# Softmax bias from a minimum of negated logits in four of five attentions

## Chip, core and metric

One NeuronCore of one Trainium2 chip runs the whole kernel. The metric is the device time of one execution in microseconds; lower is better. Three runs of the kernel before gave 2366.38, 2356.47 and 2365.3 us, median 2365.3.

## The reference

The program is two transformer blocks on 512 tokens of width 1024, all in fp32. The first has two layers: latent attention (16 heads, causal), memory cross-attention (4 heads over 256 memory rows) and a gated MLP; then sparse attention (16 heads over the best 128 keys of each query, with a bias by distance), cross-attention and the MLP again. The second block has a gated causal attention (8 heads), a pooling mixer and an MLP with a short convolution. Every attention ends in the same arithmetic for a block of 128 queries:

```
logits = q k^T * scale (+ bias), masked entries -inf
p = exp(logits - max(logits)) / sum(exp(logits - max(logits)))
out = p v
```

## The kernel before

Matrix products of weights are split in a high and a low part and made of three matmuls; they fill most of the program. Each engine has one hand-written stream of instructions, and semaphores order them. The change lies in the five attentions, which have the names `mla` (64 steps), `xa0` and `xa1` (16 steps each), `dsa` (the sparse one, 64 steps) and `fox` (the gated one, 32 steps). A step is one head and one block of 128 queries. Block 0 has 128 keys, block 1 256, block 2 384, block 3 512, so four steps in a row have four widths; the cross-attentions always have 256.

What the engines do for step i, in the order of the work:

- TensorE makes the logits in a PSUM bank (`do_logits`, up to four steps ahead; it waits for `max_done` of the step that used the bank before).
- GpSimd, in `dsa` alone, adds the bias BI and the mask MK into one of two buffers BB (L2305). Its add for step i waits for `max_done` of step i-2 (L2303).
- VectorE, in `maxima` (L1772), adds the mask (or BB) to the logits, writes the sum to the SBUF buffer PB, and reduces it to a maximum MX. This is a custom instruction, out = (in0 op0 in1) * scale with a reduction of out by op1 that starts from a given value; a short read-out instruction then writes MX and raises `max_done`.
- VectorE, in `negate` (L1777), waits for that MX, writes NM = -scale * MX and raises `negmax_done`.
- ScalarE, in `exps` (L1305), waits for `negmax_done` and computes exp(scale * PB + NM) in place, with the row sum in RS.
- VectorE takes the reciprocal RI of the sum (`invert`, L1782), waits for it and multiplies PB by it (`normalise`, L1788).
- TensorE transposes PB (`do_turn`, L775), ScalarE copies the result to SBUF, and TensorE multiplies it with the values (`do_av`, L805 or L974).

VectorE's order within a tick is: invert i, normalise i, maxima i+2, negate i+2, and then a low part of a finished head where there is one. In `dsa`, before the steps 12, 28 and 44, it also copies the keys of the next group (K_D, L2098). Each of MX, NM, RS, RI and PB has four slots, by i % 4; maxima of step i waits until the transposes of step i-4 are done, so slot i % 4 of MX is not written before the exponential of step i-4 has been used.

Of the kernel before, what the change touches and what calls it, by code (L numbers as in the profile page):

```python
# [6 lines left out]
ALU = mybir.AluOpType  # L7
ACT = mybir.ActivationFunctionType
# [7 lines left out]
S, D, MEM = 512, 1024, 256  # L16
# [15 lines left out]
TAKEN = -3.0e38  # L32
# [97 lines left out]
def build_program(nc, A, consts, out):  # L130
    ctx = ExitStack()
    with ctx:
# [32 lines left out]
        MX = keep("MX", [P, 4])  # L165
        NM = keep("NM", [P, 4])
# [162 lines left out]
        max_done = sem("max_done")  # L329
        negmax_done = sem("negmax_done")  # L330
# [68 lines left out]
        def logits_bank(name, i):  # L399
            return bank[i // 2 % 2][:, MEM * (i % 2):] if name[:2] == "xa" else bank[i % 4][:, :]  # L400
# [802 lines left out]
        def _(act):  # L1203
# [92 lines left out]
            def attention(name, groups, heads, scale, out_tile, after=None):  # L1296
                steps = 4 * heads
                s0 = STEP0[name]
                xa = name[:2] == "xa"

                def exps(g, i):
                    w = MEM if xa else P * (i % 4) + P
                    act.wait_ge(negmax_done, g * steps + (s0 + i + 1))
                    pb = PBUF[name][:, i % 4, 0:w]
                    nc.scalar.activation(pb, pb, ACT.Exp, bias=NM[:, i % 4:i % 4 + 1], scale=scale,  # L1305
                                         accum_out=RS[:, i % 4:i % 4 + 1]).then_inc(exp_done, 1)

                def evac(g, i):
                    w = MEM if xa else P * (i % 4) + P
                    act.wait_ge(turned, g * steps + (s0 + i + 1))  # L1310
                    act.wait_ge(av_done, g * steps + (s0 + i - 1))
                    copy(PTB[name][:, i % 2, 0:w], turned_bank(name, i)[:, 0:w]).then_inc(pt_done, 1)

                def outs(g, i):
                    if xa:
                        if i % 4 == 3:
                            act.wait_ge(av_done, s0 + i + 1)
                            for d in range(2):
                                out_tile(0, i // 4 * 2 + d)
                    elif i % 4 == 3:  # L1320
                        act.wait_ge(av_done, g * steps + (s0 + i + 1))
                        out_tile(g, i // 4)

                def tick(at):
                    for op, step in ((exps, at(0)), (evac, at(-2)), (after, at(-3)), (outs, at(-3 if xa else -4))):
                        if step is not None and op is not None:
                            op(*step)
                pipeline(act, groups, steps, 3 if xa else 4, 0, tick)
# [87 lines left out]
            def cross_attention(layer, stage):  # L1416
                proj_and_memory(stage, layer)
                name = f"xa_kv{layer}"

                def kv(first):  # L1420
                    def unit(i, j):
                        v = i + first
                        for k in range(2):
                            t = (TILE0[name] + 2 * j + k) % 4
                            act.wait_ge(tile_ready, v * 2 + (TILE0[name] + k + 1))
                            if first == 0:
                                dst = KX[:, bass.ds(i * 2 + k, 1), :]
                            else:
                                dst = VX[:, k, bass.ds(i * 256, 256)]
                            copy(dst, bank[t][:, 0:MEM]).then_inc(tile_free, 1)  # L1430
                        after_unit(name, v, j, v * 2 + (TILE0[name] + 2))
                    return unit

                def first_unit():
                    act.wait_ge(tile_free, TILE0[name])
                    kv(0)(0, 0)

                def next_units():
                    kv(0)(1, 1)
                    kv(0)(2, 0)  # L1440
                shift = ln(3 * layer, bank[7], later=True, amid=(first_unit, next_units))
                for v in range(3, 8):
                    first = v // 4 * 4
                    kv(first)(v - first, v % 2)
                    for c in KV_CHUNKS[v]:
                        shift(c)
                q = f"xa_q{layer}"

                def queries(i, j):
                    for k in range(2):  # L1450
                        act.wait_ge(tile_ready, i * 2 + (TILE0[q] + k + 1))
                        copy(QX[:, bass.ds(i * 2 + k, 1), :], bank[(TILE0[q] + 2 * j + k) % 4][:, :]).then_inc(tile_free, 1)
                wide_units(q, queries)
                attention(f"xa{layer}", 1, 4, (D // 4) ** -0.5, o_hi)
                for i in range(4):
                    if i in (0, 3):
                        mod_load(MOD_N * layer + i // 3)
                    after_unit(f"xa_o{layer}", i, i, TILE0[f"xa_o{layer}"] + 2 * i + 2)
                ln(3 * layer + 1, bank[7])
# [40 lines left out]
            def dsa_qi(i, j):  # L1500
                for k in range(2):
# [10 lines left out]
                 scale=float(IDXH ** -0.5)).then_inc(tile_free, 1)  # L1512
# [3 lines left out]
            for i in range(4):  # L1516
                w = P * i + P
# [65 lines left out]
                r = head_rows(hh)  # L1583
                copy(QD[r, hh // 2, :], bank[6 + hh % 2][r, :]).then_inc(o_copied, 1)
            act.sem_inc(o_copied, 2)
            attention("dsa", 1, 16, 1.0, o_copy)
            for c in range(DC):
                act.wait_ge(o_copied, 2 + HEADS)
                if c == 0:
# [63 lines left out]
                act.wait_ge(tile_free, TILE0["fox_pool"] + g + 1)  # L1653
                copy(XH[:, 4 + g, :], UF[:, g, :]).then_inc(x_hi, 1)
            after_unit("fox_pool", 0, 0, TILE0["fox_pool"] + 4)
            attention("fox", 1, 8, 0.125, head_hi)
            wide_units("fox_o", nothing)
            rms("rms2", lambda c: (tile_free, TILE0["fox_o"] + c + 1), bank[7], G2, MODC[:, 24:32], True)
            hidden(2)
# [9 lines left out]
        def _(dve):  # L1669
# [90 lines left out]
            def attention(name, groups, heads, scale, bias, out_tile, before=None):  # L1760
                steps = 4 * heads
                s0 = STEP0[name]
                xa = name[:2] == "xa"

                def maxima(g, i):
                    w = MEM if xa else P * (i % 4) + P
                    pb = PBUF[name][:, i % 4, 0:w]
                    dve.wait_ge(turned, g * steps + (s0 + i - 3))
                    in1 = bias(g, i)
                    dve.wait_ge(logits_ready, g * steps + (s0 + (i // 2 * 2 + 2 if xa else i + 1)))  # L1770
                    dve.sem_inc(logits_seen, 1)
                    nc.vector.tensor_tensor_reduce(pb, logits_bank(name, i)[:, 0:w], in1, 1.0, TAKEN, ALU.add, ALU.max,  # L1772
                                                   MX[:, i % 4:i % 4 + 1]).then_inc(max_done, 1)

                def negate(g, i):
                    dve.wait_ge(max_done, g * steps + (s0 + i + 1))
                    nc.vector.tensor_scalar(NM[:, i % 4:i % 4 + 1], MX[:, i % 4:i % 4 + 1], -scale, None,  # L1777
                                            ALU.mult).then_inc(negmax_done, 1)

                def invert(g, i):  # L1780
                    dve.wait_ge(exp_done, g * steps + (s0 + i + 1))
                    nc.vector.reciprocal(RI[:, i % 4:i % 4 + 1], RS[:, i % 4:i % 4 + 1]).then_inc(rsum_done, 1)  # L1782

                def normalise(g, i):
                    w = MEM if xa else P * (i % 4) + P
                    pb = PBUF[name][:, i % 4, 0:w]
                    dve.wait_ge(rsum_done, g * steps + (s0 + i + 1))
                    nc.vector.tensor_scalar(pb, pb, RI[:, i % 4:i % 4 + 1], None, ALU.mult).then_inc(probs_ready, 1)  # L1788

                def outs(g, i):  # L1790
                    if out_tile is None:
                        return
                    if xa:
                        if i % 4 == 3:
                            for d in range(2):
                                out_tile(0, i // 4 * 2 + d)
                    elif i % 4 == 3:
                        out_tile(g, i // 4)

                def tick(at):  # L1800
                    for op, step in ((before, at(0)), (invert, at(0)), (normalise, at(0)), (maxima, at(LAG)), (negate, at(LAG)),
                                     (outs, at(-4 if xa else -5))):
                        if step is not None and op is not None:
                            op(*step)
                for i in range(LAG):
                    maxima(0, i)
                    negate(0, i)
                pipeline(dve, groups, steps, 4 if xa else 5, LAG, tick)
# [225 lines left out]
            for i in range(NQ * IDXH):  # L2034
                qb, h = divmod(i, IDXH)
                w = P * qb + P
# [316 lines left out]
```

## Time and profile before

| what | value |
|---|---|
| median of three runs | 2365.3 us (2356.47 to 2366.38) |
| the profiled execution | 2371.9 us, span 2370.1 us |
| TensorE busy | 2256.4 us, 95% |
| VectorE busy | 1277.2 us, 54% |
| ScalarE busy | 1017.0 us, 43% |
| GpSimd busy | 185.9 us, 8% |
| granted TensorE clock, mean | 0.98 of full speed |

The span runs from the first to the last instruction of the profiled execution. PE is TensorE's matmul row, PEld its weight loads, DVE VectorE, ACT ScalarE, POOL GpSimd. Busy shares are means over stages with different limits, so a stage is read by its own window. An instruction's length in the timeline includes the time in which it was started but could not go on.

### The profile page before, as it was taken

The page shows a single profiled execution, that of the slowest core. Times are in us where ns is not written, and L with a number is a line of the kernel's source. Part 1 is how long each engine was busy: PE and PEld are TensorE (multiplying, and loading weights), DVE is VectorE, ACT ScalarE, POOL GpSimd, SP SyncE. Part 2 cuts the span into 40 slices and gives each one's busy share as a digit, 9 for nine tenths or more (in the row PEclk, how much of TensorE's full clock was granted, in tenths as well). Part 3 has the DMA queues.
Part 4 walks back from the last instruction along what each step waited for, and adds up shares of the span by engine and source line. Part 5 has one row for each costly group of instructions (what it writes and reads, how often), then busy time and mean ns, then how long its engine had stood idle before and what let it go on. Part 6 is the DMA issues. An engine that isn't in the chain of part 4 may idle for free.

```text
span 2370.1 us, 47335 instructions
## 1 busy us (share of the span) xinstructions
PE 2256.4 (95%) x18750; PEld 2137.4 (90%) x18754; DVE 1277.2 (54%) x2566; ACT 1017.0 (43%) x1576; POOL 185.9 (8%) x200
## 2 busy tenths in 40 slices
PE   7999999899999999788999899999989998999998
PEld 7978999899999888667999899999959897999997
DVE  5477544565652348998444555553254645656412
ACT  4566354433331253766354343332153535555413
POOL 1000300100000210154200100000030000000000
PEclk9999999999999999899999999999999999999999
DMA  6333341355442222000241245553212211333230
GB/s 162 76 100 89 108 142 45 89 137 156 133 151 89 80 79 83 20 1 19 72 160 63 81 116 133 136 150 104 89 45 89 77 37 54 101 94 95 100 106 36
DMA packets 303371, 219.07 MB, mean 92 GB/s; under 512 B 34379, under 2 KB 290321, under 8 KB 303249
## 3 DMA queue, kind: packets, MB, share of 16 engines
q1 hardware_dynamic: 251568, 189.32, 26.7%
q10 hardware_dynamic: 49920, 25.17, 4.1%
q0 software_dynamic: 1760, 2.88, 0.4%
q8 instruction: 87, 1.43, 0.3%
q14 instruction: 36, 0.29, 0.0%
HBM read 207.58 MB, written 2.10 MB: 88 GB/s over the span
## 4 chain that ended last, share of the span: by engine, by line
PE 85%; DVE 6%; ACT 4%; issue 2%; POOL 2%; DMA 0%; DVEq 0%; POOLq 0%; ACTq 0%; SPq 0%
PE bank L654 72%; PE bank L805 2%; PE bank L739 2%; PE bank L775 2%; PE bank L905 1%; PE bank L974 1%; POOL ZS L2239 1%; PE bank L966 1%; DVE PB_D L1772 1%; DVE M L2025 1%; PE bank L1174 1%; POOL BB L2305 1%; PE bank L1108 1%; ACT WH L617 0%; ACT XH L1208 0%
## 5 line engine op out<-in xcount | busy, mean ns | idle before, releaser
L654 PE MATMUL bank<-XH,WH 128*128 128x256 f32 x3568 | 1000.5, 280 | 32.1 <-DVE XL L1887 24.5
L654 PE MATMUL bank<-XL,WH 128*128 128x256 f32 x3568 | 997.3, 280 | 0.0
L654 PE MATMUL bank<-XH,WL 128*128 128x256 f32 x3568 | 997.0, 279 | 0.0
L654 PEld LDWEIGHTS bank<-XH,WH 128*128 128x128 f32 x3568 | 676.4, 190 | 40.6 <-issue 32.3
L654 PEld LDWEIGHTS bank<-XL,WH 128*128 128x128 f32 x3568 | 679.8, 191 | 0.2 <-issue 0.2
L654 PEld LDWEIGHTS bank<-XH,WL 128*128 128x128 f32 x3568 | 675.8, 189 | 0.0
L621 DVE TENSOR_TENSOR WL<-RAW,WH 128x2048 fp32r<-128x2048 f32 x172 | 396.5, 2305 | 514.7 <-ACT WH L617 514.7
L617 ACT ACTIVATE WH<-RAW 128x2048 fp32r<-128x2048 f32 x172 | 328.7, 1911 | 441.9 <-PE bank L654 441.8
L654 PE MATMUL bank<-HH,WH 128*128 (+1 forms) x1056 | 293.3, 278 | 0.9 <-DVE HF L1976 0.9
L654 PE MATMUL bank<-HL,WH 128*128 (+1 forms) x1056 | 293.2, 278 | 0.0
L654 PE MATMUL bank<-HH,WL 128*128 (+1 forms) x1056 | 293.2, 278 | 0.0
L654 PEld LDWEIGHTS bank<-HL,WH 128*128 128x128 f32 x1056 | 199.7, 189 | 0.0
L654 PEld LDWEIGHTS bank<-HH,WH 128*128 128x128 f32 x1056 | 198.2, 188 | 1.1 <-DVE HF L1976 1.1
L654 PEld LDWEIGHTS bank<-HH,WL 128*128 128x128 f32 x1056 | 198.2, 188 | 0.0
L1208 ACT ACTIVATE HH<-HF 128x512 f32 x66 | 41.8, 633 | 142.8 <-DVE HF L1961 107.0
L1961 DVE TENSOR_TENSOR HF<-SG,bank 128x512 f32<-128x512 f32 x44 | 30.3, 688 | 110.6 <-PE bank L654 110.6
L2220 POOL TENSOR_TENSOR ZS<-ZB 128x512 f32<-128x512 f32 x6 | 7.7, 1291 | 1020.4 <-DVE ZB L1992 754.3
L1913 DVE SCALAR_TENSOR_TENSOR ACC<-MB,CA,ACC 128x128 f32<-128x128 f32 x288 | 79.6, 345 | 0.0
L1978 DVE TENSOR_TENSOR HL<-HF,HH 128x512 f32 x66 | 45.7, 692 | 60.9 <-ACT HH L1208 60.9
L1470 ACT ACTIVATE SG<-bank 128x512 f32<-128x512 f32 x44 | 26.4, 599 | 114.1 <-DVE ACCT L1919 109.0
L1842 DVE SCALAR_TENSOR_TENSOR ZB<-XT,bank 128x512 f32<-128x512 f32 x32 | 21.9, 686 | 94.1 <-PE bank L654 94.1
L1470 ACT ACT_TABLE_LOAD x22 | 28.2, 1283 | 99.0 <-DVE ACC L1917 98.7
(311 smaller groups left out, 3255.9 us busy)
## 6 DMA issues: line engine op xcount, KB each, us to landing
RAW<-in_ffn_w_in SPq DMA_DIRECT2D x88, 512.0 KB, 5.1
MB<-in_mod_w ACTq DMA_DIRECT2D x48, 512.0 KB, 5.5
RAW<-in_ffn_w_down SPq DMA_DIRECT2D x44, 512.0 KB, 4.3
RAW<-in_ffn_up SPq DMA_DIRECT2D x44, 512.0 KB, 4.6
RAW<-in_xa_w_kv SPq DMA_DIRECT2D x32, 512.0 KB, 4.4
RAW<-in_ffn_down SPq DMA_DIRECT2D x22, 512.0 KB, 4.2
RAW<-in_xa_w_q SPq DMA_DIRECT2D x16, 512.0 KB, 3.9
RAW<-in_xa_w_o SPq DMA_DIRECT2D x16, 512.0 KB, 4.0
```

The source lines that it names most:

```text
L617: nc.scalar.activation(WH[:, par, :], RAW[:, par, :], ACT.Copy).then_inc(w_hi, 1)
L621: nc.vector.tensor_tensor(WL[:, par, :], RAW[:, par, :], f32(WH[:, par, :]), ALU.subtract).then_inc(w_split, 1)
L654: mm = nc.tensor.matmul(out_ap[:, cols], l, moving, start=(start and n == 0 and k == 0), stop=(stop and n == len(parts) - 1 and k == len(o ...
L739: nc.tensor.matmul(sq_bank[:, :], ONES, SQ[:, c % 4, :], start=(c == 0), stop=(c == DC - 1)).then_inc(sq_summed, 1)
L775: mm = nc.tensor.transpose(turned_bank(name, i)[:, P * kb:P * kb + P], pb[:, i % 4, P * kb:P * kb + P], IDN)
L805: mm = nc.tensor.matmul(o, v(hh, kb), PTB[name][:, i % 2, P * kb:P * kb + P], start=(kb == 0), stop=(kb == qb))
L905: return nc.tensor.matmul(b[:, 0:w], Q_M[hh // 2][0:NOPE + ROPE, hh % 2, P * qb:P * qb + P], K_M[0:NOPE + ROPE, hh, 0:w], start=True, stop ...
L1208: return nc.scalar.activation(dst, src, ACT.Copy, **kw)
L1470: nc.scalar.activation(SG[:, j, :], b0[:, :], ACT.Silu).then_inc(silu_done, 1)
L1913: ins = nc.vector.scalar_tensor_tensor(out=a, in0=MB[:, c, :], scalar=CA[:, c:c + 1], in1=a, op0=ALU.mult, op1=ALU.add)
L1961: nc.vector.tensor_tensor(HF[:, j, :], SG[:, j, :], b1[:, :], ALU.mult).then_inc(tile_free, 2)
L1978: nc.vector.tensor_tensor(HL[:, bass.ds(i, 1), :], HF[:, j, :], f32(HH[:, bass.ds(i, 1), :]), ALU.subtract).then_inc(hid_split, 1)
```

## The change

In all attentions but `mla` the reduction multiplies the sum by -scale instead of 1.0 and takes the minimum instead of the maximum, starting from the positive of the large constant. MX then holds -scale * max, and PB the negated scaled logits. The exponential takes MX as its bias and -1.0 as its factor, and waits for `max_done` instead of `negmax_done`. `negate` does nothing there. `mla` keeps the maximum, the negation and its wait. No buffer, no other wait and no order of other instructions is changed.

```diff
@@ -1300,9 +1300,13 @@
 
                 def exps(g, i):
                     w = MEM if xa else P * (i % 4) + P
-                    act.wait_ge(negmax_done, g * steps + (s0 + i + 1))
+                    if scale is None:
+                        act.wait_ge(max_done, g * steps + (s0 + i + 1))
+                    else:
+                        act.wait_ge(negmax_done, g * steps + (s0 + i + 1))
+                    low, by = (MX, -1.0) if scale is None else (NM, scale)
                     pb = PBUF[name][:, i % 4, 0:w]
-                    nc.scalar.activation(pb, pb, ACT.Exp, bias=NM[:, i % 4:i % 4 + 1], scale=scale,
+                    nc.scalar.activation(pb, pb, ACT.Exp, bias=low[:, i % 4:i % 4 + 1], scale=by,
                                          accum_out=RS[:, i % 4:i % 4 + 1]).then_inc(exp_done, 1)
 
                 def evac(g, i):
@@ -1451,7 +1455,7 @@
                         act.wait_ge(tile_ready, i * 2 + (TILE0[q] + k + 1))
                         copy(QX[:, bass.ds(i * 2 + k, 1), :], bank[(TILE0[q] + 2 * j + k) % 4][:, :]).then_inc(tile_free, 1)
                 wide_units(q, queries)
-                attention(f"xa{layer}", 1, 4, (D // 4) ** -0.5, o_hi)
+                attention(f"xa{layer}", 1, 4, None, o_hi)
                 for i in range(4):
                     if i in (0, 3):
                         mod_load(MOD_N * layer + i // 3)
@@ -1583,7 +1587,7 @@
                 r = head_rows(hh)
                 copy(QD[r, hh // 2, :], bank[6 + hh % 2][r, :]).then_inc(o_copied, 1)
             act.sem_inc(o_copied, 2)
-            attention("dsa", 1, 16, 1.0, o_copy)
+            attention("dsa", 1, 16, None, o_copy)
             for c in range(DC):
                 act.wait_ge(o_copied, 2 + HEADS)
                 if c == 0:
@@ -1653,7 +1657,7 @@
                 act.wait_ge(tile_free, TILE0["fox_pool"] + g + 1)
                 copy(XH[:, 4 + g, :], UF[:, g, :]).then_inc(x_hi, 1)
             after_unit("fox_pool", 0, 0, TILE0["fox_pool"] + 4)
-            attention("fox", 1, 8, 0.125, head_hi)
+            attention("fox", 1, 8, None, head_hi)
             wide_units("fox_o", nothing)
             rms("rms2", lambda c: (tile_free, TILE0["fox_o"] + c + 1), bank[7], G2, MODC[:, 24:32], True)
             hidden(2)
@@ -1769,10 +1773,14 @@
                     in1 = bias(g, i)
                     dve.wait_ge(logits_ready, g * steps + (s0 + (i // 2 * 2 + 2 if xa else i + 1)))
                     dve.sem_inc(logits_seen, 1)
-                    nc.vector.tensor_tensor_reduce(pb, logits_bank(name, i)[:, 0:w], in1, 1.0, TAKEN, ALU.add, ALU.max,
+                    negated = name != "mla"
+                    nc.vector.tensor_tensor_reduce(pb, logits_bank(name, i)[:, 0:w], in1, -scale if negated else 1.0,
+                                                   -TAKEN if negated else TAKEN, ALU.add, ALU.min if negated else ALU.max,
                                                    MX[:, i % 4:i % 4 + 1]).then_inc(max_done, 1)
 
                 def negate(g, i):
+                    if name != "mla":
+                        return
                     dve.wait_ge(max_done, g * steps + (s0 + i + 1))
                     nc.vector.tensor_scalar(NM[:, i % 4:i % 4 + 1], MX[:, i % 4:i % 4 + 1], -scale, None,
                                             ALU.mult).then_inc(negmax_done, 1)
```

## Rows read from the trace of the kernel before

**Rows 1.** The page: busy time by engine (part 1) and the chain that ended last (part 4).

```profile
PE 2256.4 (95%) x18750; PEld 2137.4 (90%) x18754; DVE 1277.2 (54%) x2566; ACT 1017.0 (43%) x1576; POOL 185.9 (8%) x200
...
PE 85%; DVE 6%; ACT 4%; issue 2%; POOL 2%; DMA 0%; DVEq 0%; POOLq 0%; ACTq 0%; SPq 0%
```

**Rows 2.** Busy time by window: first attention, a cross-attention, the sparse one, the gated one.

```profile
core 0: us, PE busy (x) PEld busy (x) DVE busy (x) ACT busy (x) POOL busy (x), PEclk, DMA share, GB/s
134.50:222.40 87.90, 86.87 (x579) 72.78 (x579) 78.10 (x329) 67.36 (x203) 0.00 (x0) 0.97 0.31 84
365.40:399.80 34.40, 32.38 (x226) 30.10 (x227) 21.55 (x87) 18.84 (x55) 0.00 (x0) 1.00 0.10 32
1011.00:1119.00 108.00, 95.23 (x594) 75.21 (x593) 101.24 (x326) 70.27 (x207) 54.66 (x62) 0.99 0.01 1
1869.00:1921.50 52.50, 49.69 (x317) 39.09 (x319) 42.87 (x170) 36.68 (x104) 0.00 (x0) 0.95 0.11 36
```

**Rows 3.** Line L775, the transposes: ns min/median/max, first to last start.

```profile
L775 PE MATMUL bank<-KC,PB_M x160: 272/273/476, 135.0 to 223.0; 128*128 128x128 f32 x160
...
L775 PE MATMUL bank<-KC,PB_D x160: 272/273/330, 1014.3 to 1118.6; 128*128 128x128 f32 x160
```

**Rows 4.** Tile NM: its instructions, and who waited for them (us, times).

```profile
L1777 DVE TENSOR_SCALAR NM<-MX x192: 153/153/156, 133.7 to 1918.5; 128x1 f32<-128x1 f32 x192
...
  ACT PB_D L1305: 38.8, 50
```

**Rows 5.** Timeline, sparse attention: start us, length us, engine, line, instruction [idle <-releaser].

```profile
1045.67 0.08 DVE L1772 DVE_READ_ACCUMULATOR2_ANT MX<- 128x1 f32 x1
1045.78 0.15 DVE L1777 TENSOR_SCALAR NM<-MX 128x1 f32<-128x1 f32 x1
...
1045.85 0.15 DVE L1782 RECIPROCAL RI<-RS 128x1 f32<-128x1 f32 x1
1045.92 1.28 POOL L2305 TENSOR_TENSOR BB<-BI,MK 128x512 f32<-128x512 f32 x1 [0.80 <-DVE MX L1772]
...
1046.04 1.24 DVE L1788 TENSOR_SCALAR PB_D<-PB_D,RI 128x128 f32<-128x128 f32 x1
...
1047.20 0.55 DVE L1772 CUSTOM_DVE_ANT_0 PB_D<-bank,BB 128x384 f32<-128x384 f32 x1
...
1047.67 0.08 DVE L1772 DVE_READ_ACCUMULATOR2_ANT MX<- 128x1 f32 x1
...
1047.94 0.46 POOL L2305 TENSOR_TENSOR BB<-BI,MK 128x128 f32<-128x128 f32 x1 [0.75 <-DVE MX L1772]
...
1048.04 0.50 DVE L1788 TENSOR_SCALAR PB_D<-PB_D,RI 128x256 f32<-128x256 f32 x1
1048.47 0.68 DVE L1772 CUSTOM_DVE_ANT_0 PB_D<-bank,BB 128x512 f32<-128x512 f32 x1
```

**Rows 6.** Groups by shape, sparse attention: count | busy us, mean ns | idle before.

```profile
L1788 DVE TENSOR_SCALAR PB_D<-PB_D,RI 128x128 f32<-128x128 f32 x16 | 16.0, 1000 | 0.6
...
L1788 DVE TENSOR_SCALAR PB_D<-PB_D,RI 128x256 f32<-128x256 f32 x16 | 7.9, 496 | 0.6
```

**Rows 7.** Groups by shape, gated attention: the same columns.

```profile
L1788 DVE TENSOR_SCALAR PB_F<-PB_F,RI 128x256 f32<-128x256 f32 x8 | 2.8, 353 | 0.3
...
L1788 DVE TENSOR_SCALAR PB_F<-PB_F,RI 128x128 f32<-128x128 f32 x8 | 2.3, 286 | 0.3
```

**Rows 8.** Timeline, sparse attention: a move of keys beside an add.

```profile
1031.80 1.82 DVE L2098 COPY K_D<-KD 64x512 f32<-64x512 f32 x2
1031.87 1.46 POOL L2305 TENSOR_TENSOR BB<-BI,MK 128x512 f32<-128x512 f32 x1 [0.80 <-DVE MX L1772]
```

**Rows 9.** Timeline: the start of the first cross-attention.

```profile
369.72 0.08 DVE L1772 DVE_READ_ACCUMULATOR2_ANT MX<- 128x1 f32 x1
...
370.03 0.43 DVE L1772 CUSTOM_DVE_ANT_0 PB_X<-bank,KC 128x256 f32<-128x256 f32 x1
...
370.52 1.59 PEld L966 LDWEIGHTS bank<-KX,QX 128*128 128x128 f32 x8 [1.81 <-DVE MX L1772]
```

## The prediction

> **What bounds the kernel now.** I read the page first: TensorE is busy for 95% of the span and makes 85% of the chain that ended last, VectorE 6% [rows 1]. A small edit on VectorE can matter only where TensorE is not the bound, so the second view is busy time by window [rows 2]. In the first attention TensorE is busy 86.9 of 87.9 us, in a cross-attention 32.4 of 34.4, in the gated one 49.7 of 52.5: TensorE's own work ends last there. The sparse attention is the exception: 95.2 of 108.0 for TensorE, 101.2 for VectorE, 54.7 for GpSimd, which works in none of the others. The transposes show its price: the first and the sparse attention have the same 64 steps and 160 transposes, but those of the first lie between 135.0 and 223.0 us (88.0), those of the sparse one between 1014.3 and 1118.6 (104.3) [rows 3]. So 16.3 us is about the most that any relief of VectorE can bring there. The four attentions that change hold 16 + 64 + 16 + 32 = 128 of the 192 negations [rows 4], half of them in the sparse one.
>
> The third view is the timeline of the sparse attention, to see what a step waits for [rows 5]. After a reduction its read-out MX starts at 1045.67. The negation follows at 1045.78, the reciprocal at 1045.85, the normalisation of 128 columns at 1046.04. That one lasts 1.24 us. GpSimd's add of the bias for a later step was released by the same MX and had started at 1045.92, 0.12 before the normalisation; it ended at 1045.92 + 1.28 = 1047.20, and the normalisation ended at 1047.28. The next reduction starts at 1047.20. It is the same with 256 columns: add 1047.94 to 1048.40, normalisation 1048.04 to 1048.54, next reduction 1048.47. The means say that this is the rule: 1000 and 496 ns in the sparse attention [rows 6], 286 and 353 in the gated one, where GpSimd is idle [rows 7]. So VectorE's 101 us hold stalls: the normalisation and the add want something that only one of them has at a time, and the one that starts first keeps it. The cycle that sets the pace is: MX, 0.25 us to the add, the whole add, 0.08 to the normalisation's end, the next reduction. The negation stands beside the 0.25 us, not in the cycle.
>
> **The change, part by part.** *Negations removed.* Each takes 0.15 us, but the reciprocal starts 0.07 behind it, since they overlap; what it holds up is the wait for MX. From MX's start to the reciprocal it is 0.18 now. Without the negation nothing between them waits for MX (the reciprocal reads the sums of an older step). The nearest spacing shown of two such short instructions is the 0.07 from negation to reciprocal, so I take 0.07 and a gain of 0.11 us of VectorE's order for each step. The bounds are 0 (the read-out holds the engine until the reciprocal starts as now) and 0.18.
>
> *Sparse attention, steady steps.* 0.11 x 64 = 7 us would be the answer if VectorE's own order set the pace. By the cycle above the normalisation only comes earlier to a stall that ends when the add ends: gain 0. What hides it is the add; if that cover goes, the next bounds are TensorE's pace. The condition is that the add still comes first. After MX the add starts at 0.25 (512 columns) and 0.27 (128 columns) [rows 5]; the normalisation comes at 0.37 now and at 0.07 + 0.19 = 0.26 then. So they start level, within 0.01. Who has it then no row shows directly. Two rows bound it: 0.12 behind, the normalisation waits [rows 5]; a copy that starts 0.07 ahead makes the add of 512 last 1.46 instead of 1.28, so it went first [rows 8]. Between these I estimate from the same rows. The adds cost 0.46 and 1.28 us for 128 and 512 columns, so 2.14 ns a column and 0.19 fixed: the add's data start at most 0.19 after its start. The stalled normalisation lost 1.24 - 0.29 = 0.95 us, so, if it could go on when the add ended, it first needed its turn at 1047.20 - 0.95 = 1046.25, that is 0.21 after its start. A common error in the end of the add shifts both alike. So VectorE asks about 0.02 later in its instruction than GpSimd, and must start some 0.02 ahead to win. It does not, narrowly. I take 0 and keep -16.3 as the other end.
>
> *Sparse attention, edges.* Before each of three key moves a copy stands where the reciprocal stands otherwise; it comes 0.11 sooner and lets its add begin sooner: 0.3. The last two steps have no add beside them: 0.2, and the last exponential is not held by the negation: 0.1. Sum 0.6, bounds 0 and 1.2.
>
> *Starts.* In a cross-attention TensorE's fifth step waits for the second reduction, which starts 0.31 after the first MX because the negation lies between [rows 9]. Four attentions x 0.11 = 0.4.
>
> *Steady steps of the cross and gated attentions.* TensorE has 2.0, 2.0 and 2.8 us free in them [rows 2], most of it at their ends: I take 0.3, bounds 0 and 3. ScalarE's exponentials wait for MX instead of NM, 0.19 sooner by the rows (1045.93 + 0.03 against 1045.75 + 0.03). It waited 38.8 us for NM in the sparse one [rows 4], but it had long finished what VectorE reads next, so this costs and gives nothing.
>
> *The reduction with a minimum and a factor that is not 1.* No row shows it. It still reads one PSUM and one SBUF operand and writes the same columns; the nearest row is its own sibling, 0.68 us for 512 and 0.55 for 384 columns [rows 5]. I take the same time. Above, a second pass over the columns at (0.68 - 0.55) / 128 = 1.0 ns each; below, nothing: the time follows the columns already. No DMA, no queue and no wait is added; the wait for MX replaces the one for NM, and behind it in ScalarE's order stands what stood there before.
>
> Sum: 0 + 0.6 + 0.4 + 0.3 = 1.3 us off the profiled execution's 2371.9 (its span is 2370.1). That execution lies 6.6 above the median 2365.3, so on the median's scale it is **2364.0**. A measurement of this kernel can tell about 0.5%, 11.8 us, from no change, and its three runs alone spread over 9.9.
>
> **The rivals.** *A. The order turns for the small add only.* The normalisation of 256 columns starts 0.26 after MX, the add of 128 beside it 0.27 after. If whoever starts first wins, it costs 0.35 instead of 0.50 and starts 0.11 sooner, 0.26 us in each of some 15 rounds of four steps, 3.9 us: 2360.1. For it: the start times. Against it: the 0.02 estimated above. The Trainium skill states this rule (SBUF — State Buffer, Who interferes with whom): VectorE and GpSimd share one port pair, and the one that issues first holds it for its whole instruction. By that rule, taken to the letter, A is the outcome; the stalls in the rows agree with the rule and leave its last 0.02 us open.
>
> *B. The order turns for all adds.* Then the normalisations cost 0.29 to 0.49 and the adds go behind them. The stall goes, but the adds come late and VectorE meets their rest in the next step, and TensorE's pace is close behind. I take half of the 16.3: 8.2, so with the edges 2355.8. For it: they start level. Against it: it needs 0.02 us of lead at the large adds, where 0.01 of lag is expected.
>
> *C, on the other side: the new reduction is slower.* It stands in the pace-setting cycle of the sparse attention. With a second pass it costs on average 320 columns x 1.0 ns = 0.33 us more, x 64 = 21 us: 2385. It decides from 0.18 us a reduction (11.8 / 64). For it: only that no row shows the form. Against it: its sibling already adds, scales and reduces in one pass.
>
> *D. Nothing reaches the end at all*, because the spacing is the read-out's own: 2365.3. It can't be told from my forecast by time, only by the trace.
>
> **How the numbers follow.** Forecast and D together 0.60, A 0.18, B 0.16, C 0.04, other 0.02. The range 2353 to 2369 takes in the forecast, A, B and D with the spread of the median, and leaves out C. Faster by over 0.5% needs B with over 11.8 of its 16.3 us: 0.07. Slower is C and a little drift: 0.04. Within: 0.89.
>
> **What would show it.** Right: L1777 has 64 instructions; the reciprocal starts 0.07 after MX; the normalisations of 128 columns still last about 1.3 us (they start earlier and end with the add); the transposes of the sparse attention still span 104. Wrong: these normalisations fall to 0.3 and the adds grow (B), only those of 256 do (A), or the reduction of 512 columns leaves 0.68 us (C). A spacing far from 0.07 would undo the order argument both ways.

## The result, and the profile after

The changed kernel took 2352.28 us (median of 19 runs, 2339.02 to 2378.91), the kernel before 2374.09 us (median of 19, 2350.78 to 2409.14). The ratio is 0.992, with a 95% interval of 0.9894 to 0.9945: faster by 0.8%, some 19 us of 2374 (13 to 25 by the interval). Ratio and interval leave out the executions that fell into a slower state of the chip (2378.91 us of the changed kernel is one), so the ratio is not quite the quotient of the two medians, 0.991. The profiled execution took 2369.5 us with a span of 2367.7, only 2.4 us less than the one of before. The stage that gained can be read from the trace, and so can much of why these two spans hide it.

The page of the kernel after, busy time by engine and the chain that ended last, against [rows 1]:

```profile
PE 2265.1 (96%) x18750; PEld 2151.4 (91%) x18754; DVE 1250.6 (53%) x2438; ACT 1017.7 (43%) x1576; POOL 190.0 (8%) x200
...
PE 88%; ACT 5%; DVE 3%; issue 2%; POOL 1%; DMA 0%; DVEq 0%; ACTq 0%; SPq 0%; POOLq 0%
```

VectorE's part of the chain is 3% where it was 6%; TensorE's rose from 85% to 88%. Next the windows of a cross-attention, the sparse and the gated attention, with the columns of [rows 2]:

```profile
366.80:401.20 34.40, 32.34 (x225) 30.05 (x226) 19.18 (x71) 19.15 (x56) 0.00 (x0) 1.00 0.10 32
1031.20:1123.00 91.80, 88.95 (x595) 74.05 (x594) 83.06 (x262) 71.75 (x207) 58.11 (x62) 0.98 0.01 1
1861.60:1914.00 52.40, 49.83 (x317) 39.14 (x319) 39.20 (x138) 36.55 (x105) 0.00 (x0) 0.95 0.11 38
```

The cross and the gated attention need what they needed (34.4 and 52.4 us here, 34.4 and 52.5 before). The window of the sparse attention is drawn here from its first reduction; TensorE is busy 89.0 of its 91.8 us. GpSimd is busy 58.1 us, where it was 54.7: its adds now hold the waits. The transposes date the stage more sharply, against [rows 3]:

```profile
L775 PE MATMUL bank<-KC,PB_M x160: 272/273/443, 135.5 to 223.1; 128*128 128x128 f32 x160
...
L775 PE MATMUL bank<-KC,PB_D x160: 272/273/329, 1034.5 to 1122.5; 128*128 128x128 f32 x160
```

In the first attention they span 87.6 us (88.0 before). In the sparse one they span 88.0 us, from 1034.5 to 1122.5, where it was 104.3. The sparse attention now runs at the pace of the first one, and these are the 16.3 us that the prediction put down as about the most that a relief of VectorE could bring (runs 7 and 8 below go 2.9 us further, without the adds).

The timeline of the kernel after shows how, against [rows 5] (start us, length us, engine, line, instruction):

```profile
1066.10 0.07 DVE L1777 DVE_READ_ACCUMULATOR2_ANT MX<- 128x1 f32 x1
1066.10 0.15 DVE L1790 RECIPROCAL RI<-RS 128x1 f32<-128x1 f32 x1
...
1066.29 0.29 DVE L1796 TENSOR_SCALAR PB_D<-PB_D,RI 128x128 f32<-128x128 f32 x1
1066.35 1.82 POOL L2313 TENSOR_TENSOR BB<-BI,MK 128x512 f32<-128x512 f32 x2 [0.80 <-DVE MX L1777]
...
1068.51 0.08 DVE L1777 DVE_READ_ACCUMULATOR2_ANT MX<- 128x1 f32 x1
...
1068.70 0.42 DVE L1796 TENSOR_SCALAR PB_D<-PB_D,RI 128x384 f32<-128x384 f32 x1
1068.77 1.91 POOL L2313 TENSOR_TENSOR BB<-BI,MK 128x256 f32<-128x256 f32 x2 [0.59 <-DVE MX L1777]
...
1069.67 1.28 DVE L1796 TENSOR_SCALAR PB_D<-PB_D,RI 128x512 f32<-128x512 f32 x1
```

The reciprocal starts with the read-out MX, not 0.07 behind it: both at 1066.10. The normalisation of 128 columns starts at 1066.29, 0.19 after MX and 0.06 ahead of the add (1066.35), and takes 0.29 us instead of 1.24. The same holds at 1068.70 for 384 columns (0.42; the add is at 1068.77). The one of 512 columns at 1069.67 still waits, 1.28 us: in its step the reciprocal comes late, after the exponential, while an add is going, and the next add starts with it at 1069.67 (the row at 1068.77 is two adds, of 256 and then 384 columns) and goes first. The groups by shape, two of the kernel before, then four of the kernel after, against [rows 6]:

```profile
L1788 DVE TENSOR_SCALAR PB_D<-PB_D,RI 128x512 f32<-128x512 f32 x16 | 17.9, 1121 | 0.6
...
L2305 POOL TENSOR_TENSOR BB<-BI,MK 128x256 f32<-128x256 f32 x16 | 11.9, 741 | 14.6 <-DVE MX L1772 14.6
```

```profile
L1796 DVE TENSOR_SCALAR PB_D<-PB_D,RI 128x512 f32<-128x512 f32 x16 | 19.6, 1227 | 0.6
...
L2313 POOL TENSOR_TENSOR BB<-BI,MK 128x256 f32<-128x256 f32 x15 | 14.1, 939 | 8.9 <-DVE MX L1777 8.9
...
L1796 DVE TENSOR_SCALAR PB_D<-PB_D,RI 128x128 f32<-128x128 f32 x16 | 8.9, 559 | 0.6
...
L2313 POOL TENSOR_TENSOR BB<-BI,MK 128x128 f32<-128x128 f32 x15 | 8.1, 538 | 8.2 <-DVE MX L1777 8.2
```

The means fell for 128 and 384 columns only, so the order turned in part of the steps. The 16 normalisations of each width in the kernel after, read one by one in the timeline:

| columns | mean before, after (ns) | what the single ones do |
|---|---|---|
| 128 | 1000, 559 | 8 lead their add by 0.06 or 0.07 us and take 0.28 or 0.29; 3 stand behind a move of keys and are free, as before; one takes 0.46; 4 start 0.01 to 0.06 behind the add and take 1.29 to 1.35 |
| 256 | 496, 489 | 7 lead by 0.08 or more and take 0.35, one has no add beside it; 8 take 0.62, because the add of 512 columns that was outrun in the step before is still going |
| 384 | 802, 421 | 15 lead by 0.06 or 0.07 and take 0.42, one has no add beside it |
| 512 | 1121, 1227 | 15 start level with an add or 0.01 behind, and wait |

The adds of 128 columns grew from 456 to 538 ns and those of 256 from 741 to 939: they wait where they were outrun; those of 384 and 512 kept their 1.0 and 1.3 us. TensorE hardly feels what is left of the stalls, as the waits show (us, times, longest; first the stage before, then after):

```profile
PEld bank L775 <- DVE PB_D L1788: 12.6, 25, 0.7
```

```profile
ACT PB_D L1309 <- DVE MX L1777: 10.2, 22, 1.5
...
PEld bank L775 <- DVE PB_D L1796: 0.2, 1, 0.2
```

TensorE's weight loads for the transposes wait 0.2 us for the normalisation; before it was 12.6 us in 25 waits. ScalarE's wait for its bias is 10.2 us, 38.8 before [rows 4].

### The profile page after: what moved, and what is told of

Same layout as the page of the kernel before. It is cut to its first block, busy times and chain, and to the rows that moved or that the text cites. A ratio compares the mean times of both kernels' runs of the same rounds, so it can differ in the third digit from the quotient of the medians.

```text
span 2367.7 us, 47207 instructions
## 1 busy us (share of the span) xinstructions
PE 2265.1 (96%) x18750; PEld 2151.4 (91%) x18754; DVE 1250.6 (53%) x2438; ACT 1017.7 (43%) x1576; POOL 190.0 (8%) x200
## 4 chain that ended last, share of the span: by engine, by line
PE 88%; ACT 5%; DVE 3%; issue 2%; POOL 1%; DMA 0%; DVEq 0%; ACTq 0%; SPq 0%; POOLq 0%
PE bank L654 73%; PE bank L805 4%; PE bank L775 2%; PE bank L739 2%; PE bank L1122 2%; PE bank L974 1%; PE bank L905 1%; POOL ZS L2247 1%; PE bank L966 1%; ACT ST L1561 1%; PE bank L1108 1%; PE bank L1174 1%; ACT XH L1208 1%; ACT WH L617 1%; ACT XT L1394 1%
```

## The experiments

Runs 1 to 8 change one thing each, and runs 9 to 11 nothing. The diffs are excerpts. The number that answers the question is the time from the first to the last start of the sparse attention's transposes (104.3 us before, 88.0 after); the ratio of times to the kernel before stands beside it with its interval.

**1. The change in the sparse attention alone.** The cross and gated attentions get their scale, maximum and negation back; a semaphore increment keeps the counts. Two lines of the edit:

```diff
-                    negated = name != "mla"
+                    negated = name == "dsa"
```

> The change in the sparse attention alone; cross and gated attentions keep maximum and negation. Theory (order at the shared resource turned in the sparse attention): its transposes span 88 us as after, and the whole gain of about 16 to 18 us is here, ratio about 0.992 to 0.993. Rival (many small savings in all four attentions, and the profile's 16 us are luck of one execution): about half the gain, ratio about 0.996.

```profile
L775 PE MATMUL bank<-KC,PB_D x160: 272/273/330, 1019.5 to 1107.6; 128*128 128x128 f32 x160
```

88.1 us, ratio 0.9933 (0.9894 to 0.9971). The whole gain of the stage is here; the interval by itself would still allow the 0.996 of the rival.

**2. The change everywhere but there.** Two lines of the edit:

```diff
-                    negated = name != "mla"
+                    negated = name not in ("mla", "dsa")
```

> The change in the cross and gated attentions alone; the sparse one is as before. Theory: the sparse transposes span 104 us as before, and the time is the same within what can be measured, 1 us or less off. Rival of many small savings: half of the gain, 8 us or more, ratio 0.996 or less.

```profile
L775 PE MATMUL bank<-KC,PB_D x160: 272/273/333, 1020.0 to 1124.7; 128*128 128x128 f32 x160
```

104.7 us, ratio 1.0012 (0.9976 to 1.0047). The 64 negations of the cross and gated attentions are worth nothing that can be measured. The theory of many small savings asked for 0.996 or less here, which the interval leaves out.

**3. No negation removed, only moved.** In the kernel before, the negation of the sparse attention stands behind the next reciprocal. Maximum, negation, its 64 instructions and ScalarE's wait for it all stay.

```diff
-                    for op, step in ((before, at(0)), (invert, at(0)), (normalise, at(0)), (maxima, at(LAG)), (negate, at(LAG)),
+                    for op, step in ((before, at(0)), (invert, at(0)), (negate if late else None, at(LAG - 1)),
+                                     (normalise, at(0)), (maxima, at(LAG)), (None if late else negate, at(LAG)),
```

> The kernel before with all its negations; in the sparse attention the negation only stands behind the next step's reciprocal instead of ahead of it, so the reciprocal can start at the read-out. Theory (only the start of the normalisation against the add counts): the normalisation starts 0.19 after MX, 0.06 ahead of the add, and the transposes span 88 us, ratio about 0.993. Rival (the work of 64 negations, or the exponential's earlier start, is what was gained): 104 us, ratio 1.000, since both are unchanged or worse here.

Its transposes, and its timeline at one step:

```profile
L775 PE MATMUL bank<-KC,PB_D x160: 272/273/330, 1016.8 to 1106.0; 128*128 128x128 f32 x160
```

```profile
1061.56 0.08 DVE L1772 DVE_READ_ACCUMULATOR2_ANT MX<- 128x1 f32 x1
1061.56 0.15 DVE L1782 RECIPROCAL RI<-RS 128x1 f32<-128x1 f32 x1
1061.67 0.15 DVE L1777 TENSOR_SCALAR NM<-MX 128x1 f32<-128x1 f32 x1
1061.74 0.29 DVE L1788 TENSOR_SCALAR PB_D<-PB_D,RI 128x128 f32<-128x128 f32 x1
1061.81 1.82 POOL L2308 TENSOR_TENSOR BB<-BI,MK 128x512 f32<-128x512 f32 x2 [0.80 <-DVE MX L1772]
1061.86 0.51 ACT L1305 ACTIVATE PB_D<-PB_D,NM 128x256 f32<-128x256 f32 x1 [0.38 <-DVE NM L1777]
```

89.2 us, ratio 0.9918 (0.988 to 0.9955). The reciprocal starts with MX at 1061.56, the negation follows at 1061.67, and the normalisation at 1061.74 is 0.07 ahead of the add. The exponential waits for NM as ever. So neither the saved work nor the earlier exponential makes the gain, but for the 1.2 us between 89.2 and 88.0 at most: the start of the normalisation does.

**4. The wait put back without the negation.** The changed kernel, with the reciprocal of the sparse attention behind the newest MX:

```diff
                 def invert(g, i):
+                    if name == "dsa":
+                        dve.wait_ge(max_done, s0 + min(i + 2, steps))
```

> The changed kernel, with one wait put back: in the sparse attention the reciprocal waits for the newest MX, as the removed negation did. No negation is in it, and the exponential still takes MX. Theory: the normalisation starts 0.30 after MX or later, 0.05 or more behind the add, and stalls for its whole length again: transposes span 104 us and the gain is gone, ratio to before about 1.000. Rival (saved work, earlier exponential): still 88 us, ratio 0.992.

```profile
1060.96 0.08 DVE L1777 DVE_READ_ACCUMULATOR2_ANT MX<- 128x1 f32 x1
1061.07 0.16 DVE L1792 RECIPROCAL RI<-RS 128x1 f32<-128x1 f32 x1
...
1061.21 0.73 POOL L2315 TENSOR_TENSOR BB<-BI,MK 128x256 f32<-128x256 f32 x1 [0.93 <-DVE MX L1777]
...
1061.27 0.89 DVE L1798 TENSOR_SCALAR PB_D<-PB_D,RI 128x384 f32<-128x384 f32 x1
```

```profile
L775 PE MATMUL bank<-KC,PB_D x160: 272/273/421, 1020.1 to 1123.3; 128*128 128x128 f32 x160
```

The reciprocal comes 0.11 after MX (1061.07 against 1060.96), the normalisation 0.31, the add 0.25. The normalisation of 384 columns takes 0.89 us, the transposes span 103.2 us, and the ratio is 0.9993 (0.9955 to 1.0031). One wait gives back 15.2 of the 16.3 us.

**5. and 6. Where the order turns.** One or two one-column instructions ahead of the reciprocal, which write a column that nothing reads in this stage:

```diff
+                    if name == "dsa":
+                        for n in range(1):
+                            nc.vector.tensor_scalar(NM[:, n:n + 1], EPS[:, 2:3], 1.0, None, ALU.mult)
                     nc.vector.reciprocal(RI[:, i % 4:i % 4 + 1], RS[:, i % 4:i % 4 + 1]).then_inc(rsum_done, 1)
```

> The changed kernel with one idle one-column instruction ahead of the reciprocal in the sparse attention. It puts the reciprocal 0.07 behind MX, where the prediction had it, and the normalisation 0.26, level with or 0.01 behind the add. Theory (only the order counts, and the forecast failed by the 0.07 alone): the normalisations of 128 columns take 1.3 us again, the sparse transposes span some 104 us, ratio to before about 1.000. Rival (the resource goes to whoever needs its data first, with a margin for VectorE): it stays at 88 us, ratio 0.992.

With one filler the timeline has:

```profile
1063.74 0.08 DVE L1777 DVE_READ_ACCUMULATOR2_ANT MX<- 128x1 f32 x1
1063.74 0.15 DVE L1792 TENSOR_SCALAR NM<-EPS 128x1 f32<-128x1 f32 x1
...
1063.81 0.15 DVE L1793 RECIPROCAL RI<-RS 128x1 f32<-128x1 f32 x1
...
1063.99 0.63 DVE L1799 TENSOR_SCALAR PB_D<-PB_D,RI 128x256 f32<-128x256 f32 x1
1064.02 0.45 POOL L2316 TENSOR_TENSOR BB<-BI,MK 128x128 f32<-128x128 f32 x1 [1.60 <-DVE MX L1777]
...
1068.53 1.35 DVE L1799 TENSOR_SCALAR PB_D<-PB_D,RI 128x128 f32<-128x128 f32 x1
1068.53 1.26 POOL L2316 TENSOR_TENSOR BB<-BI,MK 128x512 f32<-128x512 f32 x1 [0.80 <-DVE MX L1777]
```

```profile
L775 PE MATMUL bank<-KC,PB_D x160: 272/273/332, 1017.0 to 1120.2; 128*128 128x128 f32 x160
```

This is the kernel that the prediction had in mind: reciprocal 0.07 after MX, the large adds level with the normalisation (both at 1068.53). The normalisation of 128 columns takes 1.35 us, and the transposes span 103.2. The small add tells more: the normalisation of 256 columns starts at 1063.99, 0.03 ahead of the add at 1064.02, and still takes 0.63 instead of 0.35. It is no single case: 14 of the 16 normalisations of 256 columns lead by 0.02 or 0.03, and all 14 take 0.62 or 0.63. So a recorded lead of up to 0.03 us loses; in the kernel after every lead of 0.06 or 0.07 over the next add won. Between the two no run lies. The Trainium skill (SBUF — State Buffer, Who interferes with whom) has the one that issues first hold the shared ports for its whole instruction. These rows agree but for the last 0.03 us, where VectorE is recorded first and waits.

The time did not come back as fully as the stage: ratio 0.9956 (0.992 to 0.9992), where the stage's 103.2 us ask for 0.9995. The interval misses that narrowly. Run 4, with the same 103.2 us in the stage, had 0.9993; what the rest is stays open.

> Two idle instructions ahead of the reciprocal: the normalisation 0.33 behind MX, 0.07 behind the add. Both theories: the add is first, 104 us for the sparse transposes. Only a reader of the fillers' own work (0.14 us a step on VectorE, 9 us in all) would expect more than 104.

```profile
L775 PE MATMUL bank<-KC,PB_D x160: 272/273/332, 1014.9 to 1119.5; 128*128 128x128 f32 x160
```

104.6 us, with twice the idle instructions of the run above (one execution, its time is not compared). The 64 further fillers cost 1.4 us at most, where 64 times their 0.07 us would be 4.5: their own work is mostly hidden.

**7. and 8. No adds.** GpSimd only raises the semaphore; two adds at the start fill both buffers, so every step of the sparse attention adds one of these two biases, and its output is that of another bias. Of the edit, the place that drops the adds:

```diff
-                    nc.gpsimd.tensor_tensor(BB[:, i % 2, 0:w], BI[:, bass.ds(g * 4 + hh, 1), cols], MK[:, cols],
-                                            ALU.add).then_inc(bias_staged, 1)
+                    pool.sem_inc(bias_staged, 1)
```

> The kernel before, its GpSimd adds of bias and mask left out but for two at the start (every step of the sparse attention takes one of these two biases); GpSimd only raises the semaphore. All negations stay. Theory: with no add there is no stall, all normalisations take 0.29 to 0.49 us and the transposes span 88 us or less (TensorE's pace), ratio about 0.992 with the negations still in place. Rival (negations cost): well above 88.

> The changed kernel with the same adds left out. Theory: nothing is left for the change to gain: the same 88 us as the kernel before without adds, within 1 us, ratio to before about 0.992. Rival: it is several us faster than that kernel.

The transposes of the kernel before and of the kernel after, both without adds:

```profile
L776 PE MATMUL bank<-KC,PB_D x160: 272/273/327, 1019.5 to 1104.7; 128*128 128x128 f32 x160
```

```profile
L776 PE MATMUL bank<-KC,PB_D x160: 272/273/277, 1018.7 to 1103.8; 128*128 128x128 f32 x160
```

85.2 and 85.1 us: without adds the change gains 0.1 us in its best stage, and its 64 negations cost nothing there. The ratios to the kernel before (with its adds) are 0.9907 (0.9874 to 0.994) and 0.9934 (0.9901 to 0.9967). The two intervals overlap. That it is 85 and not 88 shows what the adds still cost the changed kernel: 2.9 us.

**9. to 11. The same kernels profiled again.** The spans of before and after differ by 2.4 us although one stage gained 16.3, and the sparse attention starts 20.2 us later after the change. What lies ahead of it is the same code but for the first cross-attention, which takes 34.4 us in both.

> The kernel before, unchanged, profiled once more. The profiles of before and after differ in dense stretches whose code is the same: 885 matmuls in 100 us here, 852 there. Theory (a state of the execution, not of the program): this profile has some of the same stretches at the other of the two rates, and its span differs from 2370.1 by several us, while the sparse transposes span 104 us again. Rival (the program sets it): the same stretches at the same rates as in the first profile.

> The same once more: a third draw of the rates, the sparse transposes at 104 us.

> The changed kernel, profiled once more. Theory: sparse transposes span 88 us again; the dense stretches have another mix of 885 and 852 matmuls in 100 us than the first profile of it.

Two windows of dense matmuls in three executions of the kernel before: the first profile, the second, the third. The columns are those of [rows 2].

```profile
500.00:600.00 100.00, 100.00 (x885) 100.00 (x884) 59.97 (x131) 33.61 (x32) 0.00 (x0) 1.00 0.55 148
...
1400.00:1500.00 100.00, 100.00 (x852) 100.00 (x851) 58.06 (x125) 30.58 (x31) 0.00 (x0) 1.00 0.53 141
```

```profile
500.00:600.00 100.00, 100.00 (x885) 100.00 (x884) 60.87 (x129) 32.52 (x31) 0.00 (x0) 1.00 0.53 142
...
1400.00:1500.00 100.00, 100.00 (x885) 100.00 (x884) 60.11 (x127) 33.13 (x32) 0.00 (x0) 1.00 0.53 142
```

```profile
500.00:600.00 100.00, 100.00 (x851) 100.00 (x850) 57.17 (x126) 32.33 (x31) 0.00 (x0) 1.00 0.53 142
...
1400.00:1500.00 100.00, 100.00 (x885) 100.00 (x884) 60.01 (x128) 35.11 (x34) 0.00 (x0) 1.00 0.54 146
```

TensorE is busy throughout and the granted clock is 1.00 in all six, but in 100 us it starts either 885 or some 852 matmuls. The first execution has 885 and 852, the second 885 twice, the third 851 and 885; the second and third ran on the same chip. Their spans are 2370.1, 2357.1 and 2380.2 us, with the sparse transposes at 104.3, 104.2 and 104.3. The changed kernel's second profile has a span of 2347.3 and its sparse transposes at 88.1 (1017.7 to 1105.8). Its first one has 852 matmuls in the window at 500 us and 851 in the one at 700, where the kernel before had 885 in both. From 500 to 800 us it starts 427 matmuls in each 50 us and the kernel before 444, which makes some 12 of the 20.2 us by which its sparse attention starts later; where the rest lies was not followed. So two profiles can be compared stage by stage, but not by their spans.

## Why the prediction was right and wrong

The forecast was 2364.0 us, 1.3 us less than the kernel before, as the likeliest; rival B had 2355.8. Measured are 19 us. On the scale of the forecast, 0.992 of 2365.3, that is 2346.4, and the median of the changed kernel is 2352.28: both lie under the range of 2353 to 2369. Faster by over 0.5% was given 0.07. So the forecast missed, in size and in mechanism. Point by point:

- **What bounds each stage: right.** TensorE in four attentions, and in the sparse one a cycle of MX, the add, the rest of the normalisation and the next reduction. Runs 7 and 8 show the add's part by leaving it out. The 16.3 us read from the transposes as the most were reached, 88.0 us; it is no ceiling, as 85.1 without adds shows.
- **The negation is beside the cycle: right.** Run 3 keeps all negations and has 15.1 of the 16.3 us; runs 7 and 8 differ by 0.1 us.
- **The step that failed: the spacing from the read-out to the reciprocal.** "I take 0.07 and a gain of 0.11 us", from negation and reciprocal, a pair of ordinary one-column instructions. The read-out is not such a one: what follows it without a wait starts together with it, 0.00 after. The reciprocal comes 0.18 sooner, which was the stated bound. This moved the normalisation from 0.26 to 0.19 after MX, and from level with the add to 0.06 ahead of it. So the 0 that was taken for the steady steps became 16.3 us: run 5 puts the 0.07 us back, and 15.2 of them are gone.
- **That VectorE needs a lead: right; how much: too small.** The estimate from the lengths of the adds and the stalled normalisation was 0.02 us. In run 5 leads of 0.02 and 0.03 lose; in the kernel after 0.06 is enough. The condition itself was in the text, and a spacing far from 0.07 was named as what would undo it.
- **Rival B: the right outcome at half its size.** It took half of the 16.3 because late adds would catch VectorE in the next step. They do, at 512 columns (15 of 16) and at 256 (8 of 16), but these stalls hide behind TensorE, which waits 0.2 us for them. With the spacing right and TensorE's pace as the bound, the sum would have been 16.3 + 1.3 = 17.6, inside the 13 to 25 measured.
- **Rival A fell:** in run 5 the normalisation beside the small add started ahead, as A had it, and lost.
- **Rival C fell:** the reduction of 512 columns takes 0.69 us in the sparse attention (0.68 before). **D fell** with the spacing: the trace shows 0.00, not the 0.18 of before.
- **The starts.** They were put at 0.11 us each. In the first cross-attention the second reduction now starts with the first read-out, 0.31 sooner than in [rows 9]:

```profile
371.50 0.08 DVE L1777 DVE_READ_ACCUMULATOR2_ANT MX<- 128x1 f32 x1
371.50 0.42 DVE L1777 CUSTOM_DVE_ANT_0 PB_X<-bank,KC 128x256 f32<-128x256 f32 x1
```

It is the same mis-sized spacing. If all four starts gain as much, they make 1.2 us instead of 0.4, and run 2 cannot tell that from nothing. The other small terms, 0.6 at the edges and 0.3 in the steady steps of the cross and gated attentions, no run measures either.

## What to carry to other kernels

When two engines want the same thing, a small instruction or wait can be worth next to nothing (64 negations made 0.1 us without adds) or most of a stall (15.2 us for 64 waits in run 4), and here what decided was which of them started first, by a margin. So look for instructions whose length depends on the stage (the same normalisation at 286 and at 1000 ns), lay the starts of both beside each other, and put the short one ahead by moving what stands before it. Moving the negation gave nearly what removing it gave. Take the spacing of two instructions from a pair of just those two kinds, or give the outcome on each side of it its own price.

## What was not expected of the hardware

A reduction's read-out (DVE_READ_ACCUMULATOR2_ANT, 0.08 us) holds nothing up: a reciprocal or the next reduction that does not wait for its value is recorded as starting 0.00 us after it (1066.10 and 371.50), while a reciprocal behind a one-column negation or filler starts 0.07 after that one (1063.74 and 1063.81). And TensorE has two paces in dense stretches at the same granted clock of 1.00, 885 or 852 matmuls of 256 columns in 100 us, 3.9% apart; which one a stretch gets changes from execution to execution of the same program. What sets it was not tried.
